# Two context query blocks in one score tile, and second in the group order, in layer one's attention

## What is computed

```python
# window branch (A): banded latent keys, context keys and a sink logit in one softmax
p = softmax(concat([s_band, s_ctx, sink_l]));  o = p_band @ v_band + p_ctx @ v_ctx
# dense branch (B): all latent and all context keys
p = softmax(concat([s_lat, s_ctx]));           o = p_lat @ v + p_ctx @ v_ctx
# context queries, both branches (with the sink in A): only in layers that update the context
s = einsum('bqkgd,bskd->bkgqs', qg, k_ctx) * HEAD_DIM ** -0.5
p = softmax(concat([s, sink_l]))[..., :lc];    o = einsum('bkgqs,bskd->bqkgd', p, v_ctx)
```

## Time and profile before

| | |
|---|---|
| median of three runs | 2566.09 us |
| profiled execution | 2566.4 us |
| its span on the core | 2564.6 us |
| TensorE busy in the span | 2499.2 us (97%) |
| VectorE / ScalarE / GpSimd busy | 1919.1 / 1155.4 / 734.5 us |
| attention of layer one | about 697 to 842 us of the span |

### The profile page before, as it was taken

The page is one execution under the profiler, slowest core; times in us unless marked ns, Lnnn a source line. Parts: engine busy times, 40 slices in busy tenths (PEclk is TensorE's granted clock), DMA queues, the critical chain, the costliest instruction groups (busy, mean ns, idle before and its releaser), DMA issues. The chain is left out here.

```text
span 2564.6 us, 40305 instructions
## 1 busy us (share of the span) xinstructions
PE 2499.2 (97%) x14918; PEld 2298.9 (90%) x14918; DVE 1919.1 (75%) x3244; ACT 1155.4 (45%) x2202; POOL 734.5 (29%) x659
## 2 busy tenths in 40 slices
PE   7999999999998999999999999999999999899998
PEld 4999999988888899999999889999998888899997
DVE  5888888765488488898855888888557696877776
ACT  4533433443378362433444624334345485644444
POOL 1322231223156232221231312212313254333332
PEclk8999999999999999999999999999999999999999
DMA  6344444214530124444312244453123531133332
GB/s 246 104 141 143 135 137 144 85 56 143 130 62 30 58 87 129 135 140 152 115 51 83 79 135 128 136 157 119 54 79 101 136 79 57 56 105 103 102 99 79
DMA packets 132003, 276.18 MB, mean 108 GB/s; under 512 B 15584, under 2 KB 35296, under 8 KB 130528
## 3 DMA queue, kind: packets, MB, share of 16 engines
q1 hardware_dynamic: 131808, 273.60, 34.6%
HBM read 260.43 MB, written 13.11 MB: 107 GB/s over the span
## 5 line engine op out<-in xcount | busy, mean ns | idle before, releaser
L1493 DVE TENSOR_TENSOR wlo<-raw,whi 128x512 fp32r<-128x512 f32 (+2 forms) x672 | 494.2, 746 | 300.7 <-ACT whi L986 299.6
L986 ACT ACTIVATE whi<-raw 128x512 fp32r<-128x512 f32 (+2 forms) x672 | 398.7, 605 | 375.9 <-PE ring L2007 227.8
L1902 PE MATMUL ring<-xh,whi 128*128 128x384 f32 (+1 forms) x1280 | 414.8, 324 | 12.3 <-DVE rstd L1472 6.4
L1902 PE MATMUL ring<-xl,whi 128*128 128x384 f32 (+1 forms) x1280 | 412.6, 322 | 0.0
L1902 PE MATMUL ring<-xh,wlo 128*128 128x384 f32 (+1 forms) x1280 | 412.3, 322 | 0.0
L1902 PE MATMUL ring<-th,whi 128*128 128x384 f32 (+1 forms) x960 | 309.3, 322 | 3.2 <-DVE wlo L1493 2.3
L1902 PE MATMUL ring<-th,wlo 128*128 128x384 f32 (+1 forms) x960 | 309.1, 322 | 0.0
L1902 PE MATMUL ring<-tl,whi 128*128 128x384 f32 (+1 forms) x960 | 308.4, 321 | 0.0
L1500 DVE SCALAR_TENSOR_TENSOR ada_junk<-ada_tile,row 128x1024 bf16<-128x1024 f32 x256 | 301.0, 1211 | 0.0
L658 POOL TENSOR_TENSOR raw<-raw,s_two 128x512 f32<-128x512 f32 x80 | 123.4, 1543 | 619.7 <-DVE wlo L1493 578.8
L644 POOL TENSOR_TENSOR s_one<-raw 128x512 f32<-128x512 f32 x80 | 105.5, 1319 | 547.0 <-DMA raw<-w_gu 423.6
(11 more groups left out here) (222 smaller groups left out, 5466.7 us busy)
## 6 DMA issues: line engine op xcount, KB each, us to landing
raw<-w_gu SPq DMA_DIRECT2D x352, 256.0 KB, 3.1
ada_tile<-w_turned SPq DMA_DIRECT2D x130, 512.0 KB, 3.7
raw<-w_down SPq DMA_DIRECT2D x96, 256.0 KB, 3.6
raw<-w_down SPq DMA_DIRECT2D x64, 192.0 KB, 2.5
raw<-w_in SPq DMA_DIRECT2D x48, 256.0 KB, 3.4
raw<-w_down SPq DMA_DIRECT2D x64, 128.0 KB, 2.1
raw<-w_out SPq DMA_DIRECT2D x32, 256.0 KB, 9.6
ada_first<-w_first SPq DMA_DIRECT2D x4, 1536.0 KB, 13.5
```

The source lines that it names most:

```text
L986: act.activation(weights(q, 0, cols)[0], src[:, 0:cols], ACT.Copy).then_inc(whi_ready, 1)
L1493: dve.tensor_tensor(w_l, src[:, 0:cols], w_h.bitcast(F32), ALU.subtract).then_inc(wlo_ready, 1)
L1902: last = pe.matmul(out, w, x, start=(start and k == 0 and m == 0), stop=(k == HALF - 1 and m == 2), skip_group_check=not start)
```

## The change

In layer one the order within a part becomes block 0, then a double group "4" that stands for both context blocks, then 1, 2 and 3; a part has 5 groups and layer one 60 tiles. Layer two's tiles are as before.

A double tile holds the scores of block 4 in columns 2 to 257 and of block 5 in columns 514 to 769 of one score tile of two PSUM banks, each with its own sink columns in branch A. One maximum gives two columns (`neg_max` and the row sums and reciprocals have two columns a slot now), two exponentials write to columns 2 on and 386 on of the probabilities, one reciprocal covers both, GpSimd scales the two parts with one instruction each, four transposes go in a row, and one rounded copy and one remainder take all four blocks.

The value products of a double group still give two outputs one after the other in the same bank: that of block 4 wholly in step 0, none in step 1, that of block 5 wholly in step 2. ScalarE's copy (L1155 before) and VectorE's sum (L1325 before) follow each. Outputs are counted by `s["outs"]`. GpSimd's `split_out` now comes after a tile with g = 0, 9 tiles behind (it came after g = 2, 11 tiles behind); the first output of a double group is split after a tile with g = 2. This holds for both layers.

```diff
-    blocks = 6 if layer < DEPTH - 1 else 4
-    return [(b, kv, q, g) for b in range(2) for kv in range(2) for q in range(blocks) for g in range(3)]
+    order = (0, 4, 1, 2, 3) if layer < DEPTH - 1 else range(4)
+    return [(b, kv, q, g) for b in range(2) for kv in range(2) for q in order for g in range(3)]
+def queries(q):
+    return 2 if q == 4 else 1
+def turned_blocks(b, q):
+    return 4 if q == 4 else len(key_blocks(b, q)) + 2
+def score_spans(b, q):
+    if q < 4:
+        lo = SEQ - P * len(key_blocks(b, q))
+        return [(lo, TOK, lo)]
+    return [(2, 2 + CTX, 2), (SEQ + 2, SEQ + 2 + CTX, TOK // 2 + 2)]
...
+        def outs_at(s, i):
+            k, step = divmod(i - LAG - 3, 3)
+            if not 0 <= k < len(s["tiles"]) // 3 or step == 1:
+                return []
+            mine = outs_of(s, k)
+            return [(o, (s["outs0"] + o, s["outs"][o][3])) for o in (mine[:-1] if step == 0 else mine[-1:])]
...
-                        pool.tensor_scalar(prob[:, i % P_RING, lo:TOK], prob[:, i % P_RING, lo:TOK], row_inv[:, i % 8:i % 8 + 1], 1.0,
-                                           ALU.mult, ALU.mult).then_inc(scaled_pool, 1)
-                        if g == 2 and i >= 11:
-                            split_out(i // 3 - 3, i + 1)
-                            pool.wait_ge(olo_done, s["scores"] // 3 + i // 3 - 2)
+                        for e, (lo, hi, at_p) in enumerate(score_spans(b, q)):
+                            part = prob[:, i % P_RING, at_p:at_p + hi - lo]
+                            last = pool.tensor_scalar(part, part, row_inv[:, i % 8, e:e + 1], 1.0, ALU.mult, ALU.mult)
+                        last.then_inc(scaled_pool, 1)
+                        if g == 2:
+                            k = (i - 8) // 3
+                            due = outs_of(s, k)[:-1] if k >= 0 else []
+                        elif g == 0:
+                            due = outs_of(s, (i - 9) // 3)[-1:] if i >= 9 else []
...
-                            act.activation(prob[:, i % P_RING, lo:TOK], ring[i % 2][:, lo:TOK], ACT.Exp,
-                                           bias=neg_max[:, i % 4:i % 4 + 1],
-                                           accum_out=row_sum[:, i % 4:i % 4 + 1]).then_inc(exp_done, 1)
+                            sink_col = int(b == 0)
+                            for e, (lo, hi, at_p) in enumerate(score_spans(b, q)):
+                                last = act.activation(prob[:, i % P_RING, at_p - sink_col:at_p + hi - lo], ring[i % 2][:, lo - sink_col:hi], ACT.Exp,
+                                                      bias=neg_max[:, i % 4, e:e + 1], accum_out=row_sum[:, i % 4, e:e + 1])
+                            last.then_inc(exp_done, 1)
...
-                    dve.reduce_max(neg_max[:, i % 4:i % 4 + 1], ring[i % 2][:, lo:TOK], AX.X,
-                                   negate=True).then_inc(nm_ready, 1)
+                    (lo, hi, _), pairs = score_spans(b, q)[0], queries(q)
+                    lo -= b == 0
+                    wide = ring[i % 2][:].rearrange("p (e n) -> p e n", e=2)[:, :, lo:hi] if pairs == 2 else ring[i % 2][:, lo:hi]
+                    dve.reduce_max(neg_max[:, i % 4, 0:pairs], wide, AX.X, negate=True).then_inc(nm_ready, 1)
...
-                for m in range(len(keys) * part // 3, len(keys) * (part + 1) // 3):
+                if len(mine) == 1:
+                    o, first, ms = mine[0], 0, range(len(keys) * part // 3, len(keys) * (part + 1) // 3)
+                else:
+                    o, first, ms = mine[part // 2], len(keys) * (part // 2), range(len(keys)) if part != 1 else ()
+                if part == 0 or (len(mine) == 2 and part == 2):
+                    if o >= 1:
+                        pe.wait_ge(osum_done, s["outs0"] + o)
+                for m in ms:
```

More of the change, by code:

```diff
@@ L124, in __init__ @@
                     s["tiles"] = score_tiles(layer)
+                    s["outs"], s["outs0"] = [], outs
+                    for g, (b, kv, q, _) in enumerate(s["tiles"][::3]):
+                        s["outs"] += [(g, e, b, kv, q + e) for e in range(queries(q))]
+                    outs += len(s["outs"])
                     s["release"] = [("resid_done", resid - 1), ("resid_done", resid)]
@@ L487, in shared_before, with out_counts, outs_of, outs_until @@
             tiles += list(enumerate(s["tiles"]))[:i]
[L488 to L494, removed]
+            return sum(1 for n, (b, kv, q, g) in tiles if shared_blocks(n, turned_blocks(b, q)))
+        def out_counts(s):
+            return s["outs0"] + len(s["outs"]) // 2, s["outs0"] + len(s["outs"])
+        def outs_of(s, k):
+            return [o for o, out in enumerate(s["outs"]) if out[0] == k]
+        def outs_at(s, i):
[4 more added lines that the diff above has]
+            return [(o, (s["outs0"] + o, s["outs"][o][3])) for o in (mine[:-1] if step == 0 else mine[-1:])]
+        def outs_until(s, k):
+            return s["outs0"] + sum(1 for out in s["outs"] if out[0] < k)
         block = ctx.enter_context(nc.Block())
@@ L769, in _ @@
-                    pool.wait_ge(olo_done, (s["scores"] + len(s["tiles"])) // 3)
+                        for e, (lo, hi, at_p) in enumerate(score_spans(b, q)):
[8 more added lines that the diff above has]
+                        else:
+                            due = []
@@ L770, in _ @@
+                        for o in due:
+                            assert o == split
+                            split_out(o, i + 1)
+                            split += 1
+                    for o in range(split, len(s["outs"])):
+                        split_out(o, len(s["tiles"]))
                     sum_squares(s)
@@ L1148, in _ @@
                             turned_hi(*((0, nb) if not mid else (0, mid[0]) if mid[0] else (mid[-1] + 1, nb))).then_inc(pth_done, 1)
[L1149 to L1152, removed]
+                        for o, (tr, kv) in outs_at(s, i):
                             here, there = slice(kv * HD, kv * HD + HD), slice((1 - kv) * HD, (1 - kv) * HD + HD)
                             act.wait_ge(pv_done, tr + 1)
-                            act.activation(corr[here, k // 3 % 2], bank[0][there, 0:3 * P], ACT.Copy).then_inc(corr_done, 1)
+                            act.activation(corr[here, o % 2], bank[0][there, 0:3 * P], ACT.Copy).then_inc(corr_done, 1)
                         if i < len(tiles):
@@ L1782, in scores @@
                     pe.wait_ge(stack_loaded[z % 2], 64 * (2 * layer + z // 2 + 1))
-                query = q2[:, z % 2, g, q * P:(q + 1) * P]
-                if keys:
-                    k0 = keys[0] * P
-                    edges = []
-                    if b == 0:
-                        if keys[0] == q - 1:
-                            edges.append((0, lo))
-                        if keys[-1] == q + 1:
-                            edges.append((1, SEQ - P))
-                    for part in range(2):
-                        pe.matmul(out[:, lo:SEQ], query, k2[:, z % 2, part, k0:k0 + SEQ - lo], start=(part == 0),
-                                  stop=(part == 1 and not edges))
-                    for m, (e, col) in enumerate(edges):
-                        pe.matmul(out[:, col:col + P], ident_b[:], band_mask[:, e], start=False, stop=(m == len(edges) - 1))
```

101 lines of the change are left out of this document (53 added, 48 removed).

## The result

The changed kernel takes 2575.5 us (median of six, 2572.04 to 2578.58), the kernel before 2565.8 (median of six, 2563.09 to 2567.45). The ratio is 1.0035, 95% interval 1.0025 to 1.0044: **slower by 9 us** (0.0035 of 2565.8; the two medians differ by 9.7), where I forecast 6.6 us faster, and outside my range.

A forecast was written before the change was run, and what follows sets the result against it. TensorE, busy 97% of the span, bounds the kernel; only its waits in attention could be won. Gains per part of 1.7, 2.9, 2.6 and 0.4 us, less about 1, made 6.6: from 2566.09 to 2559.5 us, range 2556.5 to 2565.0.

The forecast's parts named there:

- What this change touches is therefore the attention stretch: Layer one's attention, 697 to 842 us, TensorE busy 133.60 of 145.00 us: the only time the change could win.
- the order of GpSimd in layer two: Layer two: result splits reordered, the only change there, -0.5 to +0.5 us, taken as 0.
- rival B: Double tile's own score-bank loop sets the pace, each double step losing about 1 us: 2571.5 us, slower; chance 0.08.
- 31.7, 30.8 and 31.9: Layer one's attention: us between marks, the first value products after each part's fourth latent block, fifteen steps apart.
- Fewer chains and more cover: Attention: chains per part with a neighbour step right behind go from six to five; double steps cover more; 20 chains, not 24.
- Second place as a part of the gain: Attention, point (3): the double group comes second, so its neighbours are always latent groups and light stretches end; no separate size.
- VectorE's maximum near 0.69 us: Attention: one two-column maximum over both halves takes near 0.69 us, against 2 x 0.420 for two.
- VectorE busy some 5 us less in attention: Attention: merged maxima, remainders and reciprocals save 0.45 us of busy time per pair of tiles, 5.3 in twelve.
- the sum's two ends: VectorE's saving in attention: 5.3 us by busy time, or 2 us called certain where starts are back to back.
- rival A: Attention: VectorE sets the pace and waits only move; gain 3.0 us, 2563.1 us; chance 0.18.
- Rival C: Merged maximum costs as much as two, second place brings nothing; 1.5 us gain, 2564.6 us; chance 0.08.
- Layer two is not changed: Layer two: its marks should not move; only GpSimd's reordering reaches it, taken as 0 us.

The follow-up runs named there:

- experiment 1: Changed kernel with qkg and eps sharing one tile, so acc, rstd and the working area start at their old place: 2560.86 us against 2566.03, ratio 0.9976.
- experiment 11: Changed kernel, working area at its old place, VectorE doing a double tile's maxima, reciprocals and remainders in halves: 2561.44 us, ratio 0.9978 to the kernel before.
- experiment 9: Kernel before with layer one's groups in the order 0, 4, 5, 1, 2, 3, context tiles single, no tile moved: 2568.57 us, ratio 1.0010.
- experiment 10: Changed kernel, working area at its old place, double group last (order 0, 1, 2, 3, 4): 2560.61 us, ratio 0.9977 to the kernel before.
- experiment 3: Kernel before with qkg and eps sharing a tile, so acc, rstd and the working area start 32 bytes earlier: 2569.39 us, ratio 1.0008.
- experiment 2: Kernel before with 32 unused bytes ahead of rms, so acc, rstd and the working area start 32 bytes later: 2585.05 us, ratio 1.0070.
- Experiment 5: Separate kernel, no reference output: TensorE multiplies from sixteen tiles at 0 to 480 bytes behind a multiple of 512, VectorE idle, then busy; 384 columns 173.3 to 176.7 ns.
- experiment 8: Separate kernel: 384 columns from one tile at 128 places 32 bytes apart, weights at two places; first pass 2.88 to 2.94 us from mark to mark, second 2.88 to 2.96.
- experiment 4: Kernel before with qkg and eps in one tile, neg_max and row_sum in another, working area 64 bytes earlier: 2567.45 us, ratio 1.0005.

## Why the prediction was wrong, step by step

**The step that failed** stands in the first part: "What this change touches is therefore the attention stretch". The sum has no term for anything outside it but the order of GpSimd in layer two; what the change does to the SwiGLU stages was put at nothing, without a reason. The diff had the cause in plain sight, three tiles with a second column a slot, and I costed the instructions on them and not their place. That term is worth some +15 us: 4.9 + 5.1 + 4.9 = 14.9 in the three wide SwiGLU stages of the table, and by medians 2575.5 - 2560.9 = 14.6 between the changed kernel and experiment 1. No rival had it either; rival B, the slower one, gave the right sign for a reason that is not there.

**Attention, where the working was, held, with some luck in the number.** The marks that answer rows 4, fifteen steps apart in the changed kernel:

```profile
728.15 0.41 PE L1886 MATMUL row<-pth,v 128*128 128x384 f32 x1
...
760.11 0.41 PE L1886 MATMUL row<-pth,v 128*128 128x384 f32 x1 [0.42 <-DVE rstd L1370]
...
790.69 0.41 PE L1886 MATMUL row<-pth,v 128*128 128x384 f32 x1 [0.17 <-DVE rstd L1370]
...
823.45 0.41 PE L1886 MATMUL row<-pth,v 128*128 128x384 f32 x1
```

31.96, 30.58 and 32.76 us, where 31.7, 30.8 and 31.9 were forecast. The stage gained 7.1 where 6.6 was forecast, and with the tiles at their old place the kernel gains 0.24%, 6 us. That the numbers are so near is in part luck: 1.5 of the 7.1 us came ahead of attention, where the kernel before had a stretch at half clock and the changed one had none, and in attention 5.4 us were gained with 6.8 us at half clock. By the table behind experiment 11 the gain in attention at full clock is 7.0 to 8.7 us (159.7 against 151.0 to 152.7), inside the bounds of the sum, 4.0 and 9.6.

- *Fewer chains and more cover*: the waits bear it out. There are 24 sums as before; the waits of L1886 for them (rows 3 before) fell from 12 to 8, the longest from 1.2 to 0.6, and no value product starts over 0.8 us late:

```profile
PE row L1886 <- DVE rstd L1370: 3.2, 8, 0.6
```

  That this cover is what pays is argued from these waits and from experiment 11, which takes VectorE's savings out. No run took out ScalarE's merged copy alone (12 instructions fewer).

- *Second place as a part of the gain* (point 3): alone it brings nothing (experiment 9). On top of the double tile it is undecided: none by the medians of experiments 1 and 10, 0.7 to 2.4 us by their traces.
- *VectorE's maximum near 0.69 us*: right. Two maxima in one are

```profile
L1338 DVE TENSOR_REDUCE neg_max<-ring 128x2 f32<-128x514 f32 x6 | 4.1, 689 | 0.4 <-PE ring L1847 0.2
```

- *VectorE busy some 5 us less in attention*: 3.2 less (126.99 to 123.81 above); the whole kernel shows 6.1 less. Experiment 11 gives the merged instructions 1.4, so that of the sum's two ends for them, 5.3 and the "certain" 2 us, the low one was right and still high. The third period, that of the dense branch, 0.9 us above its forecast, is the only sign of rival A.
- *Rival B*: scores wait for an exponential three times, 1.3 us in all, where they waited five times and 1.8 before; the one such wait at a double step (0.69 us at 701.19) has its like in the kernel before at 699.07. No transpose waits for GpSimd. *Rival C*: fell with experiments 1 and 10.
- *Layer two is not changed*: right, once the clock is counted. Its mixer took 244.58 us against 242.86, but 244.60 in experiment 3, which has GpSimd's old order, and 242.93 and 242.90 in experiments 11 and 10, which have its new one. The level goes with the stretch at half clock (see the result) and not with the code.

## What to carry to other kernels

When a diff changes the size of any tile, work out what is allocated behind it and whether matmul operands move, and compare a stage that the change does not touch: if it got slower, the place is a suspect, and the change itself must be timed with the tiles held still. In a kernel that is bound by TensorE 32 unused bytes can cost 19 us of 2566 (experiment 2), so a place that is good by measurement should be pinned. Merging two small steps of a pipeline paid here, and by the waits it paid through the cover that each chain of hand-overs gets; the instructions saved on VectorE brought little. Before a difference of 1 or 2 us between two profiled stages is put down to the code, compare the granted clock in both.

## What the runs showed of the hardware

The cost of a matmul depends on the places of its moving tile and of its weights in SBUF. For 384 columns it is 173.3 to 176.7 ns, for 512 columns 226.7 to 234.2, with all other engines idle and the clock granted in full:

```profile
50.00:150.00 100.00, 100.00 (x653) 93.93 (x652) 0.00 (x0) 0.00 (x0) 1.00 0.00 1
```

(Experiment 5: stretch, length, busy PE, PEld, DVE and POOL, granted clock, DMA.) The pattern returns every 256 bytes of the moving tile's place (experiment 8). In the kernel 3 to 6 ns on the products of the moved tiles with 384 and 512 columns are enough for 19 us (experiment 2). The rule behind it was not found: neither the remainder by 64 bytes, nor the moving tile's own place, nor the distance of the two tiles alone explains all runs, and the products around one count as well or something that these runs don't separate from them (experiments 3, 4, 5 and 8).

The granted clock falls to half for short stretches that differ between executions of kernels with the same instructions. One of 3.4 us, in which TensorE is busy throughout, costs 1.7 us (layer two's mixer, 242.9 against 244.6 us).
